# POOL takes one slot's low-part subtraction and the inverse norm of kk; VectorE's products in the recurrent branch change order

## The reference

```python
w = -jax.nn.softplus(-(w0 + jnp.tanh(xw) @ w2)) - 0.5
a = jax.nn.sigmoid(a0 + xa @ a2)
g = jax.nn.sigmoid(xg) @ g2
...
kk = k * k_k.reshape(H, N).astype(jnp.float32)
kk = kk / jnp.maximum(jnp.sqrt(jnp.sum(kk * kk, axis=-1, keepdims=True)), 1e-12)
k = k * (1.0 + (a - 1.0) * k_a.reshape(H, N).astype(jnp.float32))
decay = jnp.exp(-jnp.exp(w))
...
sa = jnp.einsum('bhvk,bhk->bhv', state, -kk_t)
state = (state * w_t[:, :, None, :] + sa[..., None] * (kk_t * a_t)[:, :, None, :]
         + v_t[..., None] * k_t[:, :, None, :])
y = jnp.einsum('bhvk,bhk->bhv', state, r_t)
```

## Time and profile before

| what | value |
|---|---|
| median of 3 runs | 1711.43 us |
| lowest, highest | 1711.15 us, 1716.26 us |
| the profiled execution's own time | 1711.93 us |
| its span in the trace | 1710.0 us |
| mean granted TensorE clock | 0.947 of full speed |
| PE busy | 1577.5 us (92%) |
| DVE busy | 1026.8 us (60%) |
| ACT busy | 811.7 us (47%) |
| POOL busy | 43.6 us (3%) |

### The profile page before, as it was taken

How to read it: one execution, slowest core, us unless ns; L and a number is a source line. 1 busy time by engine, 2 the same in 40 slices (tenths; PEclk the granted TensorE clock), 3 DMA queues, 4 the chain that set the end, 5 groups by cost and what they waited for, 6 DMA issues and landing times.

```text
span 1710.0 us, 29397 instructions
## 1 busy us (share of the span) xinstructions
PE 1577.5 (92%) x10556; PEld 1436.6 (84%) x10556; DVE 1026.8 (60%) x1564; ACT 811.7 (47%) x1308; POOL 43.6 (3%) x53
## 2 busy tenths in 40 slices
PE   7898774899999999999996999999999999999997
PEld 6788573798888868999895789999899988889997
DVE  5745843598888955555543755555555554655554
ACT  6423432477677744333443454333433345653332
POOL 1120000000000000000000100000000000000000
PEclk9898787899999999999997599999999999999999
DMA  6312694399979966555452055555455544155552
GB/s 248 111 62 78 113 107 141 134 348 348 350 255 352 346 227 222 184 184 184 148 185 74 0 185 194 187 185 186 148 186 186 185 163 149 47 176 185 184 184 74
DMA packets 83846, 308.03 MB, mean 180 GB/s; under 512 B 9278, under 2 KB 9406, under 8 KB 83648
## 3 DMA queue, kind: packets, MB, share of 16 engines
q1 hardware_dynamic: 79632, 289.97, 48.8%
q0 software_dynamic: 3856, 16.98, 5.3%
q10 hardware_dynamic: 288, 0.12, 0.0%
HBM read 299.69 MB, written 7.34 MB: 180 GB/s over the span
## 4 chain that ended last, share of the span: by engine, by line
PE 84%; DVE 8%; ACT 4%; DMA 2%; issue 1%; POOL 0%; SPq 0%; DVEq 0%; POOLq 0%; ACTq 0%
PE ps L1478 24%; PE ps L1479 23%; PE ps L1480 23%; PE ps L1484 3%; PE ps L1607 2%; DMA raw<-in_wstream 2%; DVE w_lo L907 2%; PE ps L1579 1%; PE ps L1667 1%; PE ps L1742 1%; ACT arena L590 1%; DVE xT_lo L946 1%; ACT w_hi L536 1%; ACT xT_hi L609 1%; PE ps L1823 1%
## 5 line engine op out<-in xcount | busy, mean ns | idle before, releaser
L907 DVE TENSOR_TENSOR w_lo<-raw,w_hi 128x1024 fp32r<-128x1024 f32 x549 | 646.6, 1221 | 286.3 <-ACT w_hi L536 284.7
L536 ACT ACTIVATE w_hi<-raw 128x1024 fp32r<-128x1024 f32 x549 | 549.3, 1055 | 240.2 <-PE ps L1480 190.4
L1478 PE MATMUL ps<-xT_hi,w_hi 128*128 128x256 f32 x1656 | 470.5, 284 | 4.5 <-DVE xT_lo L946 3.7
L1479 PE MATMUL ps<-xT_lo,w_hi 128*128 128x256 f32 x1656 | 468.8, 283 | 0.0
L1480 PE MATMUL ps<-xT_hi,w_lo 128*128 128x256 f32 x1656 | 468.8, 283 | 0.0
L1478 PEld LDWEIGHTS ps<-xT_hi,w_hi 128*128 128x128 f32 x1656 | 317.6, 192 | 10.4 <-issue 6.9
L1479 PEld LDWEIGHTS ps<-xT_lo,w_hi 128*128 128x128 f32 x1656 | 317.7, 192 | 3.2
L1480 PEld LDWEIGHTS ps<-xT_hi,w_lo 128*128 128x128 f32 x1656 | 317.7, 192 | 0.0
L1478 PE MATMUL ps<-w_hi,xT_hi 128*128 128x256 f32 (+2 forms) x848 | 263.1, 310 | 21.7 <-DVE w_lo L907 20.1
L1479 PE MATMUL ps<-w_lo,xT_hi 128*128 128x256 f32 (+2 forms) x848 | 252.8, 298 | 0.0
L1480 PE MATMUL ps<-w_hi,xT_lo 128*128 128x256 f32 (+2 forms) x848 | 252.6, 298 | 0.0
(11 more groups left out here) (311 smaller groups left out, 1324.9 us busy)
## 6 DMA issues: line engine op xcount, KB each, us to landing
raw<-in_wstream SPq DMA_DIRECT2D x549, 512.0 KB, 5.0
bias_tiles<-arena POOLq DMA_DIRECT2D x2, 3072.0 KB, 51.3
arena<-bias_tiles POOLq DMA_DIRECT2D x2, 3072.0 KB, 14.6
const<-in_const POOLq DMA_DIRECT2D x1, 1112.0 KB, 7.7
x_res<-in_x SPq DMA_DIRECT2D x2, 512.0 KB, 4.3
arena<-in_mem POOLq DMA_DIRECT2D x1, 1024.0 KB, 5.5
out<-arena SPq DMA_DIRECT2D x2, 512.0 KB, 2.7
smallw<-in_smallw POOLq DMA_DIRECT2D x1, 768.0 KB, 39.1
```

Source lines behind the costliest of these rows:

```text
L536: nc.scalar.activation(w_hi[:, slot, lo:hi], raw[:, slot, lo:hi], ACT.Copy).then_inc(S_(f"hi_{part_}"), 1)
L907: tt(w_lo[:, slot, lo:hi], raw[:, slot, lo:hi], w_hi[:, slot, lo:hi].bitcast(F32), ALU.subtract).then_inc(S_(f"lo_{part_}"), 1)
L1478: a = mm(out_, stat_[0], mov[0], start=start, stop=False)
L1479: b = mm(out_, stat_[0], mov[1], start=False, stop=False)
```

## The change

The subtraction for slot QKV0 leaves VectorE and goes to POOL, in three pieces. ACT copies the sums of squares instead of taking their root. POOL puts a floor of 1e-24 under them and raises them to the power -0.5, 128 x 512 elements, which gives the inverse norm; VectorE's floor and reciprocal are gone. On VectorE all that doesn't need the norm (`kp`, `rw_rk`, the products of r with e1, `rw_k`) now stands ahead of the wait for it (`rw_kkinv`). Before VectorE splits slot QKV0 + 1 it waits for POOL's count.

```diff
--- before.py
+++ after.py
@@ -468,6 +468,17 @@
             pool.dma_start(posi[:, 0:S], pos_in[0:1, :].rearrange("a s -> (a s)").partition_broadcast(P)
                            ).then_inc(S_("pos_loaded"), 16)
             pool.dma_start(posi[:, S:S + T], pos_cols_in).then_inc(S_("pos_loaded"), 16)
+
+            for part_, (lo, hi) in PIECES.items():
+                pool.wait_ge(S_(f"hi_{part_}"), QKV0 + 1)
+                pool.wait_ge(S_(f"lo_{part_}"), QKV0)
+                nc.gpsimd.tensor_tensor(w_lo[:, QKV0 % 2, lo:hi], raw[:, QKV0 % 2, lo:hi],
+                                        w_hi[:, QKV0 % 2, lo:hi].bitcast(F32), ALU.subtract).then_inc(S_(f"lo_{part_}"), 1)
+            pool.wait_ge(S_("rw_kknorm"), 1)
+            nc.gpsimd.tensor_scalar(two["sq"], two["sq"], 1e-24, None, ALU.max).then_inc(S_("kk_floor"), 1)
+            pool.wait_ge(S_("kk_floor"), 1)
+            nc.gpsimd.tensor_tensor(two["tmp"], two["sq"], minus_half.unsqueeze(2)[:, :, 0:1].broadcast_to([P, 2, S]),
+                                    ALU.pow).then_inc(S_("rw_kkinv"), 1)
 
             pool.wait_ge(S_("l1t_ready"), 2)
             pool.wait_ge(S_("elem_done"), 1)
@@ -739,7 +750,7 @@
             split_all(QKV0)
             proj(RW0 + 2)
             act.wait_ge(S_("rw_kksum"), 1)
-            nc.scalar.activation(two["sq"].rearrange("p j s -> p (j s)"), ps[:, 3, :], ACT.Sqrt).then_inc(S_("rw_kknorm"), 1)
+            nc.scalar.activation(two["sq"].rearrange("p j s -> p (j s)"), ps[:, 3, :], ACT.Copy).then_inc(S_("rw_kknorm"), 1)
             nc.scalar.activation(g_tok.rearrange("p t s -> p (t s)"), ps[:, 2, :], ACT.Copy).then_inc(S_("g_ready"), 1)
             act.wait_ge(S_("rw_cum"), 1)
             for j in range(2):
@@ -1163,7 +1174,6 @@
             link(ins)
             tt(two["sq"], two["kk0"], two["kk0"], ALU.mult).then_inc(S_("rw_kksq"), 1)
             link(shift(0, 1))
-            split_all(QKV0)
             dve.wait_ge(S_("lam_exp"), 1)
             link(tt(nlam, lame[:, 1:2], lame[:, 0:1], ALU.subtract))
             link(ts(nlam, nlam, -LAM_INIT, None, ALU.add))
@@ -1189,25 +1199,28 @@
             dve.wait_ge(S_("evacuated"), evac_until(RW0 + 2))
             link(shift(4, 5))
 
-            dve.wait_ge(S_("rw_kknorm"), 1)
-            link(ts(two["sq"], two["sq"], 1e-12, None, ALU.max))
-            link(nc.vector.reciprocal(two["tmp"], two["sq"]))
-            tt(two["kkn"], two["kk0"], two["tmp"], ALU.mult)
             for j in range(2):
                 ins = ts(two["kp"][:, j, :], two["a"][:, j, :], 1.0, pc("k_a")[:, j:j + 1], ALU.subtract, ALU.mult)
             link(ins)
             link(stt(two["kp"], two["kp"], 1.0, k_, ALU.add, ALU.mult))
             for j in range(2):
                 stt(rw_rk[:, j, :], r_[:, j, :], pc("r_k")[:, j:j + 1], two["kp"][:, j, :], ALU.mult, ALU.mult)
+            dve.wait_ge(S_("rw_exp"), 1)
+            for c in range(T):
+                w = slice(P * c, P * c + P)
+                tt(rw_ar[:, :, c, 1, :], r_[:, :, w], two["e1"][:, :, w], ALU.mult)
+            tt(rw_k, two["kp"], two["e2"], ALU.mult)
+            dve.wait_ge(S_("rw_kkinv"), 1)
+            link(tt(two["kkn"], two["kk0"], two["tmp"], ALU.mult))
             link(tt(two["b"], two["kkn"], two["a"], ALU.mult))
             dve.wait_ge(S_("rw_exp"), 1)
             for c in range(T):
                 w = slice(P * c, P * c + P)
                 tt(rw_ar[:, :, c, 0, :], two["kkn"][:, :, w], two["e0"][:, :, w], ALU.mult)
-                tt(rw_ar[:, :, c, 1, :], r_[:, :, w], two["e1"][:, :, w], ALU.mult)
-            tt(rw_b, two["b"], two["e2"], ALU.mult)
-            tt(rw_k, two["kp"], two["e2"], ALU.mult).then_inc(S_("elem_done"), 1)
-            split_all(QKV0 + 1)
+            tt(rw_b, two["b"], two["e2"], ALU.mult).then_inc(S_("elem_done"), 1)
+            for part_ in PIECES:
+                dve.wait_ge(S_(f"lo_{part_}"), QKV0 + 1)
+                split_lo(QKV0 + 1, part_)
 
             for c in range(T):
                 if c:
```

## The result

| what | before | after |
|---|---|---|
| median | 1711.29 us (4 runs, 1710.38 to 1716.26) | 1787.47 us (4 runs, 1783.63 to 1807.35) |
| the profiled execution's own time | 1711.93 us | 1787.96 us |
| its span | 1710.0 us | 1786.1 us |
| mean granted TensorE clock | 0.947 | 0.931 |

The ratio to before is 1.0469, with a 95% interval from 1.0441 to 1.0498: slower by 76 us. The forecast was slower, by 127.5 us, in a range from 1716 to 1848 us.

A forecast was written before the change was run, and what follows sets the result against it. VectorE's chain up to elem_done was taken to bound this stage, TensorE idle meanwhile. The profiled 1711.9 us + 0.3 (turns and delayed exponentials using up the 7.2 saved) + 127.2 for the power = 1839.4 us; range 1716 to 1848.

The forecast's parts named there:

- a chain on VectorE sets this stage, and that `elem_done` counts one for one: From 40.9 to 59.5 us VectorE's chain holds TensorE idle for 6.74 us; any shift of elem_done moves the end equally.
- The turns between POOL and VectorE in the three pieces: From 40.8 to 48.35 us POOL's subtractions and VectorE's operations alternate, each blocking the other fully; the 7.2 us saved are used up.
- piece d: POOL's last subtraction, ready at 48.35 us, 1.4 late for TensorE's side jobs; these end at 54.2, hidden before elem_done.
- X: Duration of POOL's power on 128 x 512, starting at 49.75 us; between 1.8 and 127.2 us, taken as 127.2.
- upper reading: The power's excess over an addition belongs to the elements: 248 ns each, 127.2 us for 512 columns.
- pipelined: Rival: the power's columns overlap, 512 cost 5 to 60 us; total 1717 to 1772 us, chance 0.36.
- short powers: Rival with turns: the power takes 1.8 to 4.8 us; total 1714.0 to 1717.0 us, chance 0.15.
- VectorE waits for the whole power: The fourth running sum and all VectorE work behind it wait for the power's end; elem_done comes 10.0 us after that.
- the full price: Likeliest case: every column of the power pays fully; 1839.4 us, own range 1797 to 1848, chance 0.42.
- The faster rival: A short power and no turns: elem_done 5.1 us earlier, TensorE's clock kept at 1.00; 1702.3 us, chance 0.07.
- side remark on the clock: With TensorE idle under 1 us, the clock stays 1.00 and its work from 59.6 to 70 us shrinks by up to 4.5.
- The saving on ACT: Copies need no table load, so ACT saves one of 1.28 us; the one before the exponentials stays.

The follow-up runs named there:

- e2: The changed kernel without POOL's subtractions: VectorE splits slot QKV0 again, POOL has only the floor and the power; 1783.8 us against 1711.1, ratio 1.0420.
- e1: The changed kernel without the power: ACT's square root and VectorE's floor and reciprocal return, POOL keeps the subtractions; 1714.3 us against 1711.6, ratio 1.0022.
- e5: The kernel before, with unused powers of widths 1 to 128 in POOL's idle time; 1716.14 us in a single execution.
- e4: The changed kernel with POOL's power on only 128x256, the other half of the inverse norm set to 0.003; median 1764.7 us, power 41.38 us.
- e8: The kernel before, with 30 unread products on TensorE while it waits for elem_done; 1709.1 us against 1713.2, ratio 0.9978.

## Why the prediction was right or wrong

**That a chain on VectorE sets this stage, and that `elem_done` counts one for one: right.** 75.3 us later there, 76.1 in the span.

**The turns between POOL and VectorE in the three pieces: right.** Piece a from 40.89, the last piece's end at about 48.2 (predicted 48.35), the one-column operation (L1178 of the new file) held up to 43.4, the sums stretched to 5.84 us. TensorE did wait for piece d: its step k = 5 started at 48.33, as predicted hidden. The power started at 49.84 (predicted 49.75), and that the two agree so closely is luck in part: POOL's floor took 1.60 us (1.50 in e2), where 0.7 was taken and 1.27 was held to be the most, but the running sums ran beside it, where the prediction had put the second ahead of it, the third behind it and the fourth behind the power. By e1, the subtractions on POOL are a loss of about 3 us and not the gain of 3.4 that their removal from VectorE promises.

**The step that failed in size: X.** It took the whole excess of the power over an addition, 496 ns for two elements, as cost of the elements: 248 ns each, 127.2 us. The runs show 159 ns a column and 0.3 to 0.6 us fixed, so 82.2 us. Of the 713 ns of the earlier trace rows 0.32 us are the columns' and 0.4 us the instruction's, 0.18 more than the addition's 0.217: that is about a third of the excess, and just the case from which the prediction worked out the lower end of its own range (X = 85). It chose the upper end, as it had no row at a second width and found nothing that spoke for a fixed share; the power of one more width would have settled it, as e5 did. The "upper reading" of a price known at one size is an upper bound, and should have been used as one. The reading that a column has a full price of its own, and that 512 columns don't overlap, was right, since the price from 2 to 64 columns is that from 256 to 512; both pipelined and short powers are out.

**The step that failed in kind: that VectorE waits for the whole power.** The prediction let the fourth running sum, and with it all that VectorE had left, stand behind the power, 10.0 us of work after its end. It was 2.8: only what needs the inverse norm. The fourth sum ended at 49.46, before the power began, and the power shut VectorE out for 0.6 us at its start. ACT's exponentials, expected 2.0 us after the power's end, ran beside it:

```profile
51.84 0.40 ACT L760 ACTIVATE arena<-arena,stat 128x128 f32<-128x128 f32 x1 [4.67 <-DVE stat L1197]
```

The step was carried over from the masks of the earlier trace rows and from the Trainium skill's page "SBUF — State Buffer", section "Who interferes with whom", which says that whoever issues first gets the shared pair for the whole instruction, and the other fully blocks. For subtractions and masks the traces agree (L1178 with 2.25 us); for a power they don't (0.6 of 82 us), and the measurement decides. What seems to count is the time in which POOL reads its operands. For it speaks that the wait ended 1.27 us after the power's start with 512 columns and 0.84 us after it with 256 (e4); that is an inference from these durations, and no run tried it by itself.

The two errors add up: 127.2 - 82.2 = 45.0, and 10.0 - 2.8 = 7.2; 127.5 - 52.2 = 75.3 us. The measured 1787.5 us lies in no single case's range: the full price had 1797 to 1848, the pipelined power 1717 to 1772. That it lies in the stated range is owed to the width by which that range took in both, and not to the sum.

**The faster rival** (no turns, a short power) fell in both of its conditions. Its side remark on the clock holds: e8, in which TensorE isn't idle, gained 4.1 us, where 4.5 was the most.

**The saving on ACT** (a table load less) was there, and worth nothing: ACT's exponentials waited 4.67 us for `rw_cum`, as the turns had made that late.

## What to carry to other kernels

A price per instruction that was read at two columns is no price for 512: fit a line through two widths before a wide operation is moved to an engine, and POOL's power, at 159 ns a column, is for columns of statistics only. Work that POOL takes over from VectorE comes back as waits if VectorE has operands in SBUF at the same time; count the turns, not the busy time (3.4 us of work taken away and 6.2 us of waits, in e1). If an inverse norm has to leave VectorE, the logarithm and the exponential on ACT did it here for two activations of 0.6 us and two table loads of 1.28, as many loads as the square root and the exponentials had needed.

## What the runs showed of the hardware that was not expected

- POOL's power on 128 x n: 713 ns, 10.5, 20.7, 41.4 and 82.2 us for n = 2, 64, 128, 256 and 512, on one line although VectorE was busy beside that of 128 columns and idle beside most of that of 512.
- A power on 128 x 512 keeps an operation of VectorE with two inputs out for 0.6 us at its start, one on 128 x 256 for 0.18 us, a subtraction on 128 x 1024 for nearly all of its 2.4 us (2.1 us).
- Some executions of a kernel lose 18 to 20 us at once. In the one that was profiled TensorE's clock was 0.50 for 20 us and 0.58 to 0.72 around them, in an attention stage where it is 0.91 to 1.00 otherwise, 1400 us behind the place of the edit. A comparison of a few us needs enough executions to see this.
